# Whole values of h from the accumulators, one gate tile moved from the opening to attention

## The reference

```python
h = rms_norm(x, norm_w)
proj = jnp.einsum('bsd,de->bse', h, w_in)
qa, ka, va, za, qb, kb, vb, zb, ab, bb, gate = jnp.split(proj, split_points, axis=-1)
ya = diff_attention(qa, ka, va, q_gain, k_gain, lam_qk, out_gain, lambda_init) * silu(za)
ob = gated_deltanet(qb, kb, vb, ab, bb, conv_w, a_log, dt_bias)   # conv, decay, 64-token chunks
yb = rms_norm(ob, gdn_norm_w) * silu(zb)
gates = sigmoid(gate.reshape(B, S, 2, D_MODEL))
merged = gates[:, :, 0] * (ya @ w_up_da) + gates[:, :, 1] * (yb @ w_up_gdn)
x = x + merged @ w_out
```

## Time and profile before

| | us |
|---|---|
| median of 3 runs | 951.08 (950.0 to 951.36) |
| the profiled execution | 950.83 |
| its span, first to last instruction | 948.7 |
| TensorE busy in it | 913.1 (96%) |
| VectorE, ScalarE, GpSimd busy | 654.4, 409.3, 352.7 |

### The profile page before, as it was taken

The page is one execution under the profiler, slowest core; times in us unless marked ns, Lnnn a source line. Parts: engine busy times, 40 slices in busy tenths (PEclk is TensorE's granted clock), DMA queues, the critical chain, the costliest instruction groups (busy, mean ns, idle before and its releaser), DMA issues.

```text
span 948.7 us, 14533 instructions
## 1 busy us (share of the span) xinstructions
PE 913.1 (96%) x5147; PEld 747.5 (79%) x5147; DVE 654.4 (69%) x1467; ACT 409.3 (43%) x844; POOL 352.7 (37%) x262
## 2 busy tenths in 40 slices
PE   7868999999999999999999999999999989999998
PEld 5656888887787887888887878888787778888887
DVE  6968488887427666766667355757667667655995
ACT  6244455544442442333433346556554562122441
POOL 4638556653443112222223333323223123223652
PEclk9979999999999999999999999999999989999999
DMA  6052222116222122121112300100100003334603
GB/s 228 23 180 60 83 56 67 45 45 211 89 56 67 56 68 66 58 66 56 36 46 68 101 23 23 35 23 23 34 24 23 23 23 111 101 115 166 227 1 133
DMA packets 77134, 69.73 MB, mean 74 GB/s; under 512 B 4402, under 2 KB 62988, under 8 KB 77068
## 3 DMA queue, kind: packets, MB, share of 16 engines
q1 hardware_dynamic: 74828, 66.76, 22.6%
q10 hardware_dynamic: 2240, 2.12, 0.8%
HBM read 54.70 MB, written 14.17 MB: 73 GB/s over the span
## 4 chain that ended last, share of the span: by engine, by line
PE 84%; DVE 6%; POOL 3%; issue 2%; ACT 2%; DMA 2%; SPq 0%; ACTq 0%; DVEq 0%
PE PS L1613 14%; PE PS L1615 14%; PE PS L1617 14%; PE PS L1736 5%; PE PS L1737 5%; PE PS L1738 5%; PE PS L2026 3%; PE PS L2146 3%; PE PS L2147 3%; PE PS L2148 3%; PE PS L2001 3%; PE PS L2019 1%; ACT prob L1417 1%; DVE conv_out L2260 1%; PE PS L1857 1%
## 5 line engine op out<-in xcount | busy, mean ns | idle before, releaser
L1613 PE MATMUL PS<-h_hi,w_hi 128*128 128x512 f32 x512 | 209.2, 409 | 14.5 <-POOL w_lo L857 9.5
L1617 PE MATMUL PS<-h_hi,w_lo 128*128 128x512 f32 x512 | 208.9, 408 | 0.0
L1615 PE MATMUL PS<-h_lo,w_hi 128*128 128x512 f32 x512 | 207.8, 406 | 0.0
L857 POOL TENSOR_TENSOR w_lo<-w_raw,w_hi 128x512 fp32r<-128x512 f32 x66 | 93.3, 1415 | 300.0 <-ACT w_hi L1050 293.0
L1613 PEld LDWEIGHTS PS<-h_hi,w_hi 128*128 128x128 f32 x512 | 97.6, 191 | 33.9 <-POOL w_lo L857 11.5
L1617 PEld LDWEIGHTS PS<-h_hi,w_lo 128*128 128x128 f32 x512 | 97.4, 190 | 17.8 <-issue 1.0
L1615 PEld LDWEIGHTS PS<-h_lo,w_hi 128*128 128x128 f32 x512 | 97.4, 190 | 17.7 <-issue 0.7
L2335 DVE SCALAR_TENSOR_TENSOR conv_out<-pre,half_conv,conv_out 128x1024 f32<-128x1024 f32 x36 | 64.9, 1802 | 9.3 <-ACT conv_out L1130 8.4
L1050 ACT ACTIVATE w_hi<-w_raw 128x512 fp32r<-128x512 f32 x68 | 42.6, 629 | 55.4 <-PE PS L1617 45.4
L2657 DVE TENSOR_REDUCE mx<-PS 128x1 f32<-128x1024 f32 (+7 forms) x64 | 48.4, 756 | 20.2 <-PE PS L2006 19.8
L1417 ACT ACTIVATE prob<-PS,nm,r_qk 128x1024 f32<-128x1024 f32 (+7 forms) x64 | 52.6, 829 | 16.7 <-DVE nm L2661 16.7
(11 more groups left out here) (343 smaller groups left out, 2189.5 us busy)
## 6 DMA issues: line engine op xcount, KB each, us to landing
w_raw<-in_w_in SPq DMA_DIRECT2D x82, 256.0 KB, 2.9
x_in<-in_x SPq DMA_DIRECT2D x8, 512.0 KB, 7.8
s_raw_slots<-in_w_in SPq DMA_DIRECT2D x16, 256.0 KB, 2.8
zv<-gate_dram SPq DMA_DIRECT2D x8, 512.0 KB, 3.9
out_sb<-in_x SPq DMA_DIRECT2D x4, 1024.0 KB, 12.6
out<-out_sb SPq DMA_DIRECT2D x16, 256.0 KB, 2.2
gate_dram<-gate_st SPq DMA_DIRECT2D x6, 512.0 KB, 2.9
z_dram<-stg SPq DMA_DIRECT2D x4, 512.0 KB, 2.8
```

The costliest lines, as they stand in the source:

```text
L857: pool.tensor_tensor(lo[:, b, :], w_raw[:, b, :], hi[:, b, :].bitcast(F32), ALU.subtract)\
L1613: pe.matmul(dst, w, hi, start=first, stop=False)
L1615: pe.matmul(dst, w, lo, start=False, stop=False)
L1617: mm = pe.matmul(dst, lo_w, hi, start=False, stop=last)
```

## The change

- **Whole quarters.** ACT now makes F12 and F22 by reading the transposed x in PSUM once more with the norm's scale (`h_whole(n)`, n = 8 to 15, eight ACTIVATEs). Two last transposes of the opening wait for it. DVE makes F11 (between the last `rest_of_h`) and F21 (after S2). POOL makes none; its eight L894 instructions are gone.
- **Gate tile.** Gate tile 1 leaves the opening. It becomes the first of B_FILL, whose tiles each move on by one; (GB, 2) goes to C_FILL, which now has 12 tiles. The numbers behind it change: G_VA is 2, G_FILL is 6. The 48 filler steps are spread over C_STEPS and C_FIRST. In B_AT the steps from X on stand 1 or 2 places later.
- **Loads.** W21 and W22 of the first pair are loaded at once; W11 and W12 follow the first gate tile's splits, with the stores of h between them.
- **Order.** ACT forms W11 of the first pair between T1 and T2, W12 between the gate tile's two takes. The transposed parameter vectors are made within the gate tile. `channel_parameters` and two memsets go behind the first pair's sums; the lambda sums and unit rows stand ahead of `z_tile(0)` on DVE; the two exponentials go to the value stage on ACT.
- **Value stage.** G_VA's slabs are loaded as soon as their places are free in the last pair, the next tile's ahead of the reloads of zv; its `split_hi` stands within the last pair.

The core of the diff:

```diff
-        G_AB, G_GATE, G_VA, G_FILL = 0, 1, 3, 7
+        G_AB, G_GATE, G_VA, G_FILL = 0, 1, 2, 6
...
-        B_FILL = [(GA, 2), (GA, 3), (GA, 4), (ZA, 0), (GA, 5), (GA, 6), (ZA, 1), (GA, 7), (GB, 0), (ZA, 2), (GB, 1), (GB, 2), (ZA, 3),
+        B_FILL = [(GA, 1), (GA, 2), (GA, 3), (ZA, 0), (GA, 4), (GA, 5), (ZA, 1), (GA, 6), (GA, 7), (ZA, 2), (GB, 0), (GB, 1), (ZA, 3),
                   (QK, 1, 0), (QK, 0, 0)]
...
-        B_AT = {"state": 0, "products": 4, "v_new": 6, "update": 10, "X": 48, "Y4": 52, "X4": 56, "V4": 59, "out": 59,
-                "Y5": 63, "V5": 66, "Y6": 70, "V6": 73}
+        B_AT = {"state": 0, "products": 4, "v_new": 6, "update": 10, "X": 50, "Y4": 54, "X4": 58, "V4": 61, "out": 61,
+                "Y5": 65, "V5": 68, "Y6": 71, "V6": 74}
...
-        C_QT, C_S_FIRST, C_V_FIRST, C_FIRST = 3, 7, (10, 15), 24
-
-        C_STEPS = ({7: (2, 9, 10), 6: (2, 8, 9), 5: (1, 8, 8), 4: (1, 7, 8), 3: (1, 6, 9), 2: (1, 6, 8), 1: (2, 5, 8), 0: (2, 5, 9)},
-                   {7: (2, 8, 8), 6: (2, 8, 6), 5: (1, 7, 5), 4: (1, 6, 5), 3: (1, 5, 5), 2: (1, 5, 4), 1: (1, 4, 3), 0: (2, 3, 0)})
+        C_QT, C_S_FIRST, C_V_FIRST, C_FIRST = 3, 7, (10, 15), 26
+
+        C_STEPS = ({7: (2, 9, 12), 6: (2, 8, 10), 5: (1, 8, 9), 4: (1, 7, 9), 3: (1, 6, 10), 2: (1, 6, 9), 1: (2, 5, 9), 0: (2, 5, 11)},
+                   {7: (2, 8, 9), 6: (2, 8, 7), 5: (2, 7, 6), 4: (1, 7, 6), 3: (1, 6, 6), 2: (1, 6, 5), 1: (2, 5, 4), 0: (2, 6, 0)})
...
-            pool.wait_ge(h_lo_ready.sem, h_lo_ready.at(2 * NK - 1))
-            split_lo(G_GATE, 0)
-            for k in range(4):
-                h_whole(F22, k)
-            split_lo(G_GATE, 1)
-            for k in range(4):
-                h_whole(F21, k)
             for b in range(2):
-                split_lo(G_GATE + 1, b)
+                split_lo(G_GATE, b)
...
-            for n in range(6, 2 * NK):
+            def h_whole(n):
+
+                half, k = n // NK, n % NK
+                act.wait_ge(h_lo_ready.sem, h_lo_ready.at(n))
+                act.activation(f_parts[:, (F11, F21, F12, F22)[n // 4], k % 4, :], PS[:, h_bank(n), :], ACT.Copy,
+                               scale=vec[:, 48 + k:49 + k]).then_inc(t_f.sem, 1)
+
+            for n in range(6, 12):
                 round_h(n)
+            h_whole(8)
+            h_whole(9)
...
+                        if p == N_PAIRS - 1:
+                            for b in range(2):
+
+                                q = max(q for q in range(7 * N_PAIRS) if q % SLOTS == b)
+                                act.wait_ge(f_used.sem, f_used.at(q // 7, q % 7 + 1))
+                                split_hi(G_VA, b)
                         after_sixth(p)
...
             take(gate_tile, 36)
+            pe.wait_ge(t_f.sem, t_f.at(7))
+            vec_transpose()
             ab_transposes()
             whole(gate_tile)
-            whole(projection(G_GATE + 1, G_GATE + 1))
...
-                        pe.wait_ge(proj_out.sem, proj_out.at(G_GATE + 1))
+                        pe.wait_ge(proj_out.sem, proj_out.at(G_GATE, 1))
...
-            for n in range(7, 2 * NK):
+            for n in range(7, 12):
                 rest_of_h(n)
-            channel_parameters()
+            dve.wait_ge(xT_ready.sem, xT_ready.at(12))
+            for k in range(2):
+                h_whole(F11, k)
+            rest_of_h(12)
+            rest_of_h(13)
+            for k in range(2, 4):
+                h_whole(F11, k)
+            rest_of_h(14)
+            rest_of_h(15)
...
             for k in range(4):
-                h_whole(F11, k)
-                h_whole(F12, k)
-                if k > 0:
-                    t_difference(1, k - 1)
-            t_difference(1, 3)
+                t_difference(1, k)
             for k in range(4):
                 t_difference(2, k)
                 t_rest(1, k)
-            for name in S_SUMS[:3]:
+            for name in S_SUMS[:2]:
                 weight_sum(0, name)
+            for k in range(4):
+                h_whole(F21, k)
             for k in range(4):
                 t_difference(4, k)
                 t_rest(2, k)
...
+            lambda_sums()
+            units()
             z_tile(0)
             stage(1)
```

More of the change, by code:

```diff
@@ L633, in hybrid_block @@
         t2_sum = conv_flat[:, 0:2 * SEQ].rearrange("p (k n) -> p k n", k=4)
-        F11, F12, F21, F22 = range(4)
+        F11, F21, F12, F22 = range(4)
         def t_sum(n, k):
@@ L757, in _ @@
                 sp.dma_start(zv[:, j, :], z_dram[j * P:(j + 1) * P, :]).then_inc(z_loaded.sem, 16)
-            for j in range(1, HEADS):
+            for j in range(2, HEADS):
                 load_tile(G_VA + j, COL_VA + j * P)
@@ L1605, in second_half @@
                 pe.wait_ge(h_lo_ready.sem, h_lo_ready.at(k + 2))
+                if k >= 6 and pair == 0:
+                    pe.wait_ge(t_f.sem, t_f.at(k - 6))
                 for t in range(first, first + 2):
@@ L1719, in product_of @@
                         pe.wait_ge(quarter_out.sem, quarter_out.at(p - 2, 4))
+                if i == 1 and p == 0:
+                    pe.wait_ge(proj_out.sem, proj_out.at(G_GATE))
                 over = {6: "X1", 3: "Y5", 7: "X2"}
@@ L2251, in _, with h_whole @@
-            dve.reduce_sum(even_odd[:, :], block_of[:, :].rearrange("p (q e) -> p e q", e=2), AX.X).then_inc(units_ready.sem, 1)
-            dve.wait_ge(h_lo_ready.sem, h_lo_ready.at(2 * NK - 1))
-            for n in range(2):
-                dve.memset(pre[n][:, 0:TAPS - 1], 0.0).then_inc(pre_zero.sem, 1)
-            def h_whole(quarter, k):
-                toks = {F11: T0, F12: T1}[quarter]
-                dve.tensor_tensor(f_parts[:, quarter, k, :], h_hi[:, k, toks].bitcast(F32), h_lo[:, k, toks].bitcast(F32),
-                                  ALU.add).then_inc(t_f_dve.sem, 1)
+            def h_whole(quarter, k):
+                ks = {F11: 0, F21: 4}[quarter]
+                dve.wait_ge(h_lo_ready.sem, h_lo_ready.at(ks + k))
+                dve.tensor_tensor(f_parts[:, quarter, k, :], h_hi[:, ks + k, T0].bitcast(F32), h_lo[:, ks + k, T0].bitcast(F32),
+                                  ALU.add).then_inc(t_f_dve.sem, 1)
@@ new lines, in _, with lambda_sums @@
+            for n in range(7, 12):
+                rest_of_h(n)
+            dve.wait_ge(xT_ready.sem, xT_ready.at(12))
[7 more added lines that the diff above has]
+            rest_of_h(15)
+            def lambda_sums():
+                dve.wait_ge(lam_loaded.sem, 16)
+                for i in range(2):
+                    if i:
+                        dve.wait_ge(lam_sums.sem, 1)
+                    dve.tensor_tensor_reduce(lam_junk[:, :], lam_rows[:, 2 * i, :], lam_rows[:, 2 * i + 1, :], 1.0, 0.0,
+                                             ALU.mult, ALU.add, lam_s[:, i:i + 1]).then_inc(lam_sums.sem, 1)
@@ L2371, in _ @@
                     weight_sum(p + 1, "S4")
+                if p == 0:
+                    channel_parameters()
+                    for n in range(2):
+                        dve.memset(pre[n][:, 0:TAPS - 1], 0.0).then_inc(pre_zero.sem, 1)
+                    dve.wait_ge(pre_zero.sem, 2)
+                    dve.wait_ge(vec_ready.sem, 5)
                 if kind == CONV:
@@ L2453, in _ @@
             z_tile(1)
+            dve.wait_ge(lam_exp.sem, 1)
+            dve.tensor_tensor(neg_lam[:, :], lam_s[:, 3:4], lam_s[:, 2:3], ALU.subtract).then_inc(lam_ready.sem, 1)
+            dve.wait_ge(lam_ready.sem, 1)
+            dve.tensor_scalar(neg_lam[:, :], neg_lam[:, :], -LAMBDA_INIT, None, ALU.add).then_inc(lam_ready.sem, 1)
             with dve.Fori(2, HEADS) as j:
```

172 lines of the change are left out of this document (83 added, 89 removed).

## The result

| | before | changed |
|---|---|---|
| median, us | 950.54 (947.89 to 951.36, 4 runs) | 939.45 (938.67 to 940.67, 4 runs) |
| span of the profiled execution | 948.7 | 937.4 |
| TensorE busy | 913.1 | 909.4 |

The ratio is 0.9887, with a 95% interval from 0.9867 to 0.9907: 10.7 us faster, between 8.8 and 12.6. The forecast was 943.6, 7.5 us under the 951.08 known then, and its range, 938 to 949, holds the time; the narrower 941 to 946, to which it gave a chance of 0.50, does not.

What follows compares the result with a forecast made beforehand. TensorE was taken as the bound, busy 913.1 of 948.7 us, losing time to waits and half clock. Gains of 2.2, 1.3, 1.3 and 2.7 summed to 7.5 us, giving 943.6 us, range 938 to 949.

Steps and rivals of the forecast that it cites:

- Opening: Up to product 3 of the first pair: reached sooner by more than the 11.0 us of moved matmuls; gain 2.2 us.
- the shared budget: In the opening, DVE and POOL contend, so the sum of their work counts; a pair takes about 1.7 us.
- Value stage: Waits of 1.5 and 1.2 us ahead of the first two value tiles go, a new one comes; gain 1.3 us.
- The new wait: In the value stage, TensorE would wait 1.3 to 1.4 us for POOL's w_lo of the second slab.
- B stage: Later steps from X on shorten the 1.9 us stall to 1.45 and remove two short ones; gain 1.3 us.
- Attention: Extra filler steps shorten stalls (1.4), another tile costs net 0.1, the clock may stay up (1.4); gain 2.7 us.
- even odds: At the end of attention, the clock stays up with even chance, counted as half of 2.9 us.
- (a): Opening's stall only moves, value stage gives nothing, clock still falls at attention's end; about 948 us, chance 0.18.
- (c): DVE's back-to-back differences in the opening shut POOL out, product 3 comes no sooner; slower, 956.5 us, chance 0.07.
- (b): All goes well: product 6 starts at 63 and the clock stays up in attention; about 938 us, chance 0.15.
- (d): Gate tile 1's steps displace softmax chains in attention and bring new stalls; 950.5 us, no change, chance 0.10.
- signs of being wrong: Product 6 after 70, over 2 us ahead of product 3, value-stage half clock, or new projection-tile waits within attention.

Runs made afterwards that it cites:

- first experiment: Changed kernel with F12 and F22 made by POOL again (eight tensor_tensors) instead of by ACT; 945.15 us.
- sixth experiment: Changed kernel with tmp_X taken ahead of T3's roundings, plus products 1 and 2 on free weight slots and F11 behind the last h_lo; 937.10 us.
- tenth experiment: Changed kernel with the first two value tiles' loads and the first one's split back in their old places; 941.20 us.
- eighth experiment: Changed kernel with only B_AT as before, the steps from X on one or two filler places earlier; 941.88 us.
- fourth experiment: Kernel before, with only the filler-step numbers of the last head's last two query blocks changed; 949.86 us, ratio 1.0002.
- second experiment: Changed kernel with gate tile 1 back in the opening, with the old filler lists, B_AT, C_FIRST and C_STEPS; 942.92 us.
- eleventh: Changed kernel with gate tile 1 and the small parameters in the opening, tmp_X ahead of T3's roundings, new B_AT, old C_STEPS; 933.80 us.

## Why the prediction was right, and where it was off

**Opening, forecast 2.2, measured 2.7.** The mechanism held step by step. DVE's differences start at 32.70 (32.5), the last of T3 ends at 63.9, product 6 starts at 65.13 (66.5), product 3 at 70.41 (71.2), its wait is gone. The first experiment bears out the shared budget. Two sizes were off. The wait ahead of product 6 is 6.5 us, not 12, since TensorE was not there at 54.5 but at 58.6: its gate tile began at 33.4, lost 1.7 us to half clock (33.4 to 36.8, behind a wait of 1.7 us for h_lo), and it waited 1.7 ahead of product 2, where the form of W12 must wait for the gate tile's end and POOL's part of it took 3.47 us beside DVE's run:

```profile
49.17 3.47 POOL L905 TENSOR_TENSOR w_lo<-w_raw,w_hi 128x512 fp32r<-128x512 f32 x1 [5.43 <-ACT w_hi L1124]
```

None of that cost anything: product 6 waited for tmp_X longer than all of it, and when the sixth experiment removed it, the time did not fall. And the half clock behind product 6's wait covers 5.8 us of matmuls, 2.9 us lost, not 1.9, so that of the 1.4 us by which product 6 starts sooner than forecast 0.8 are left at product 3. The step that was missing is a cause: I took tmp_X's place behind T3's roundings as given and asked how soon DVE and POOL could be done. The wait was there for the queue's order, and reordering it was worth more (3.6) than this term.

**Value stage, forecast 1.3, measured 2.25.** The removed waits were right, and the tenth experiment ties them to the loads and the split. The new wait was 0.47, not 1.4: the term of 4.2 us for the small DVE instructions was mis-sized, since I took it from rows where POOL worked beside them. They took 1.3.

**B stage, forecast 1.3, measured 1.55.** Right in cause and size; in the eighth experiment 1.6 in stalls.

**Attention, forecast 2.7, measured 1.2 in stalls and 3.0 of clock.** The sum was low because I gave the clock even odds and it stayed up, in all eight profiles with the new C_STEPS; with the old ones it fell in three of four. The reason that I gave, stalls shortened to 0.2 and 1.0, was wrong: they are 0, 1.22 and a new one of 1.05. I had counted three steps ahead of each wait where there was one or two, and had not seen that the old half clock hid a stall. And 3.0 is the clock's length, not what it is worth. From the last scores on, the old program took 183.02 us with the fall and 182.41 at full clock, and the fourth experiment showed no gain from that place alone. The changed kernel takes 181.96 there with eight filler steps (1.8 us) more, 2.9 us less than the kernel before for the same work. So of these 2.9 the clock alone gives 0.6; the rest came with the filler steps that now stand there.

**Rivals.** (a) was half right: the stall moved, but shrank. (c), POOL shut out by DVE's run, shows in one instruction (3.47 us) and did not decide anything, as POOL had gaps to catch up in. (b) came nearest in the result, 938, by other terms. (d) did not come: the only new waits of projection matmuls in attention are 0.43 and 0.57 us, where one of 0.93 stood before; such waits were on the list of signs of being wrong, but in sum these are no longer than the old one. (In (c), the opening's cost where product 3 starts at 77 is 5.5 by its own terms, not 5.8, which changes nothing.)

**What stays open.** How much of the 10.7 us is the moved tile: with the queues as changed it was 3.5 (second experiment), with both orders mended 1.8, not told from nothing (eleventh). What the clock gave to each difference of medians, since it fell in some executions and not in others of the same kernel. And why the clock falls in one execution behind the same wait and not in another.

## What to carry to other kernels

Where an instruction waits, ask first what stands ahead of it in its own queue: product 6 waited 6.5 us for a copy that began at 64.49, though the last matmul of its operand had run at 50.69, because four roundings that it did not need came before. Price DVE's instructions by rows where POOL is quiet or busy as it will be at the new place, and count what both have to do as one sum. Work taken off that sum (eight instructions to ACT) pays in full where TensorE waits for it; work moved off TensorE pays only what it fills elsewhere.

## What was new about the hardware

- Some small DVE instructions suffer from POOL more than large ones in proportion: a sum of 64 columns took 1.41 us beside POOL and 0.21 to 0.23 without it, a 128x128 tensor_scalar 0.85 and 0.22, a 128x512 tensor_tensor 1.69 and 0.60. The first and the last lose 1.2 and 1.1 us, nearly the 1.27 of a POOL instruction alone. Others did not suffer: the two tensor_reduces of the unit rows took 0.36 and 0.27 us beside POOL and 0.37 and 0.28 without it.
- The clock does not answer a wait the same way in each execution. Behind the 1.90 us wait at the head of the B stage it stayed at full in the kernel before and fell in three other kernels; behind the 1.46 us wait of the changed kernel it stayed up in five profiles and fell in two. The kernel before spread over 947.2 to 954.4 us in 21 runs and the fourth experiment, also with the 1.90 us wait, over 948.4 to 954.4 in 10; the first experiment, with the 1.46 us one, over 944.4 to 945.7 in 10. That the waits make the spread is not shown.
- A fall of the clock can cost less than its length, since work beside TensorE catches up: at the end of attention 6.8 us of half clock cost 0.6 us, because a stall of 1.6 us appeared when the clock stayed at full.
